# Splitting the experts' weight pieces in one operation per engine, in place of two halves

## The chip, the cores and the metric

One core of one Trainium2 chip runs the whole program. The metric is device time in microseconds (us), the median of several runs. The reader needs five engines' names: TensorE (PE, with its weight loads shown apart as PEld), VectorE (DVE), ScalarE (ACT), GpSimd (POOL) and SyncE (SP), which issues the weight loads from HBM.

## What is computed

The reference is two small transformer models, one after the other, on 256 tokens of width 1024, all in fp32. Each has two layers of mixing (recurrences and several attentions) and feed-forward. What matters here is the last feed-forward, a mixture of 8 experts with two experts per token:

```python
out = jnp.zeros_like(t)
for e in range(N_EXPERTS):
    out = out + combine[:, e:e + 1].astype(t.dtype) * swiglu(t, wg[e], wu[e], wd[e])
```

with `swiglu(x, wg, wu, wd) = (silu(x @ wg) * (x @ wu)) @ wd`; `wg` and `wu` are 1024 x 3584 and `wd` is 3584 x 1024 per expert. The kernel gathers each expert's tokens (at most 128) and so reads all 8 experts' weights once.

## The kernel before, in words

**Pieces.** All weights of the program are cut into 565 pieces of at most 128 partitions x 2048 columns (1 MB), in the order of use (`plan`). The experts' pieces are 336 of them: for each expert 7 groups of 512 hidden columns, and for each group two pieces "g" (gate), two pieces "u" (up) and two pieces "d" (down, of the group before). Their key begins with "moe".

**Precision.** TensorE multiplies fp32 operands as high and low parts. ScalarE copies a piece into `WH` (the high part, fp32r; line 1670 of the kernel), VectorE subtracts it from the raw piece into `WL` (the low part; line 2250), and TensorE makes three products for each block (`mm3`, lines 772 to 774): high by high, low by high, high by low. A piece of an expert takes 12 matmuls of 512 columns. The inputs are `XTH`/`XTL` for "g" and "u", and `HTH`/`HTL` for "d".

**Buffers and queues.** `WH` and `WL` hold WR = 3 pieces each. The raw pieces have 5 slots (`raw`), and 5 more lent ones (in `AR`) during the experts. SP issues the load of a slot's next piece when the second half of `WL` of the slot's last piece is made (line 598).

**The order on each engine.** Every engine runs its instructions in the order in which they were written. A helper, `Lane`, writes the split of piece i+2 where the engine comes to piece i (`take`), as two halves: `split(i, 0)` and `split(i, 1)`, each with its own wait and its own increment of the semaphores `wh` and `wl`. In the experts' part the two halves always stand one behind the other. ScalarE's first half waits for the landed load and for `wdone(i-3)`, TensorE's last matmul on the buffer that it overwrites. VectorE's half waits for the same half of `WH`. TensorE waits for `wl(i, 0)` ahead of a piece and for `wl(i, 1)` ahead of its second part.

**What stands between the splits.** In group i of the experts, ScalarE and VectorE have besides:
- ScalarE copies the transposed hidden block into `HTH` (L2068), ahead of the split of a second "u" piece; VectorE subtracts for `HTL` (L2914).
- ScalarE's Silu of the gate (L2092), ahead of the split of a first "d" piece; VectorE's product with the up part (L2941), ahead of the split of a first "g" piece.
- once per expert, `put_back` (L2072 on ScalarE, L2919 on VectorE), which takes an expert's result from PSUM; and `prep` of the next expert, whose two sets of four small copies (L2051 on ScalarE, L2893 on VectorE) make its `XTH` and `XTL`.
- in the last expert, after groups 3 and 5, `unfold` on VectorE (L2876): two operations of 128x1024 that add the gathered sums to `X`.
- in the first expert, the places of the rows (a string of tiny VectorE operations, L2841 to L2850 among them).

Of the kernel before, what the change touches and what calls it, by code (L numbers as in the profile page):

```python
# [7 lines left out]
F32 = mybir.dt.float32  # L8
# [4 lines left out]
ALU = mybir.AluOpType  # L13
# [8 lines left out]
WR = 3  # L22
# [6 lines left out]
class Sig:  # L29
# [9 lines left out]
    def inc(self, *key):  # L39
        assert self.keys[self.n] == key, (self.sem.name, self.keys[self.n], key)  # L40
        self.n += 1
        return self.sem, 1


    def part(self, name):

        return Part(self, name)
# [193 lines left out]
def program(nc, dr, cf, cb, ci, out):  # L241
    ctx = ExitStack()
    with ctx:
        def sb(name, shape, dt=F32):
            return ctx.enter_context(nc.sbuf_tensor(name, shape, dt))

        def sem(name):
            return ctx.enter_context(nc.semaphore(name))

        def sig(name, *keys):  # L250

            if len(keys) == 1 and isinstance(keys[0], list):
                return Sig(sem("s_" + name), keys[0])
            return Sig(sem("s_" + name), itertools.product(*[range(k) if isinstance(k, int) else k for k in keys]))
# [3 lines left out]
        WH = sb("WH", [P, WR, 2048], F32R)  # L258
        WL = sb("WL", [P, WR, 2048], F32R)
# [126 lines left out]
        for l in range(2):  # L386
            for key, ap, n in ((("n1", l), dr["norm1_g"], 8), (("n2", l), dr["norm2_g"], 8), (("nm", l), dr["norm_mix_2"], 8),
# [3 lines left out]
                if key != ("n1", 0):  # L391
                    k = sum(v[1] for v in rows.values())
# [11 lines left out]
        PIECES = plan(dr)  # L404
# [8 lines left out]
        slots = [raw[:, i, :] for i in range(RAW)] + lent  # L413


        ld_w = [sem(f"ld_w{s}") for s in range(RAW + LENT)]
        wh = sig("wh", NP, 2)
        wl = sig("wl", NP, 2)
        wdone = sig("wdone", NP)
        tops = {("m1", 0), ("m1", 1), ("m2", 0)}  # L420
        tdone = sig("tdone", [(i,) for key, i in sorted(final.items(), key=lambda x: x[1])
                              if key[0] != "moe" and (key[0] not in tops or key[1] != "d" or key[2] == (5 if key[0][0] == "m2" else 7))])
# [1233 lines left out]
        def scalar():  # L1656
            act = nc.scalar
            own = Own(sem("a_step"))

            def split(i, h):  # L1660
                s, k, _, _ = HOME[i]
                m = PIECES[i][2] * PIECES[i][3]
                c = slice(h * m // 2, (h + 1) * m // 2)
                if i == 0:
                    act.wait_ge(*((ld_w[s], 16) if h else (ld_h, 16)))
                elif h == 0:
                    act.wait_ge(ld_w[s], 16 * k)
                    if i >= WR:
                        act.wait_ge(*wdone.at(i - WR))
                act.copy(WH[:, i % WR, c], slots[s][:, c]).then_inc(*wh.inc(i, h))  # L1670

            lane = Lane(PIECES, split)

            def half(key, h, gains, hi=XTH, nch=4, b0=6, only=(0, 1)):
# [155 lines left out]
            for r in range(2):  # L1830
                half(("n1", 0), 0, gain4(("n1", 0), 0), only=(r,))
                split(0, r)
            half(("n1", 0), 1, gain4(("n1", 0), 1), b0=0)
            split(1, 0)
            split(1, 1)
            norm(("n1", 0), (ld_x, 16), (ld_y, 16))
# [11 lines left out]
            for l in range(2):  # L1848
# [32 lines left out]
                for t in range(T):  # L1881
                    m = act.activation(XN[:, t, :], XN[:, t, :], ACT.Sigmoid)
# [5 lines left out]
                for t in range(T):  # L1888
                    m = act.activation(ZB[:, t, :], ZB[:, t, :], ACT.Sigmoid)
# [351 lines left out]
        def vector():  # L2241
            dve = nc.vector
            own = Own(sem("v_step"))

            def split(i, h):
                s, _, _, _ = HOME[i]
                m = PIECES[i][2] * PIECES[i][3]
                c = slice(h * m // 2, (h + 1) * m // 2)
                dve.wait_ge(*wh.at(i, h))
                dve.tensor_tensor(WL[:, i % WR, c], slots[s][:, c], WH[:, i % WR, c].bitcast(F32), ALU.subtract).then_inc(*wl.inc(i, h))  # L2250

            lane = Lane(PIECES, split, True)

            def half(key, h, gains, hi=XTH, lo=XTL, nch=4, b0=6, only=(0, 1)):
# [250 lines left out]
            for r in range(2):  # L2505
                half(("n1", 0), 0, gain4(("n1", 0), 0), only=(r,))
                split(0, r)
            half(("n1", 0), 1, gain4(("n1", 0), 1), b0=0)
            split(1, 0)
            split(1, 1)  # L2510
            lane.cut = 2
# [703 lines left out]
```

## Time and profile before

| what | value |
|---|---|
| time, median of 3 runs | 2423.18 us (2423.03 to 2423.38) |
| profiled execution, span from first to last instruction | 2422.9 us |
| TensorE busy | 2397.3 us, 99% of the span |
| VectorE busy | 1753.7 us, 72% |
| ScalarE busy | 1493.6 us, 62% |
| experts' part | about 1437 to 2386 us |
| moved from and to HBM | 612 MB, mean 253 GB/s |

The profile puts each instruction under its line and engine. "Busy" of TensorE is modelled and includes the tail of each matmul, which overlaps the next. The mean of an operation (in ns) is from its start to its acknowledged end, and operations queued back to back overlap by about 0.1 us. "Idle before" is the time in which an engine had nothing running ahead of an instruction, with what released it. The granted clock is the share of 2.4 GHz that TensorE had.

### The profile page before, as it was taken

To read this page: it belongs to the slowest core of one execution; us is meant where nothing else is said; L and a number is where in the kernel's file an instruction comes from. 1 tells how busy PE (TensorE), PEld (TensorE's weight loads), DVE (VectorE), ACT (ScalarE), POOL (GpSimd) and SP (SyncE) were. 2 spreads that over 40 slices of the span, in tenths; PEclk is the share of its full clock that TensorE was granted. 3 is DMA by queue.
4 is the path that set the end of the run, shared out by engine and by line. 5 is a ranking of instruction groups with operands and counts; after the bars stand their busy time and mean duration, and the time that the engine had idled before them with its cause. 6 is when DMAs were issued, how large, how long until landed. Compare 5 with 4: busy or idle time off the path is not lost.

```text
span 2422.9 us, 30793 instructions
## 1 busy us (share of the span) xinstructions
PE 2397.3 (99%) x12268; PEld 2028.3 (84%) x12268; DVE 1753.7 (72%) x2133; ACT 1493.6 (62%) x1951; POOL 85.0 (4%) x106
## 2 busy tenths in 40 slices
PE   9999999999999999999999999999999999999998
PEld 7888899888888998888888888888888888888887
DVE  5655655566456556565455579999999999999997
ACT  5445544544454445554446667787777777877776
POOL 0000000000000000110000200000000000000000
PEclk9999999999999999999999999999999999999999
DMA  8453575544546555345555369999999999999992
GB/s 302 143 175 123 173 253 186 186 157 142 171 139 197 191 183 166 122 162 190 165 184 173 122 250 389 394 389 379 385 379 384 380 385 377 384 380 379 380 389 97
DMA packets 267984, 612.10 MB, mean 253 GB/s; under 512 B 12424, under 2 KB 17526, under 8 KB 267836
## 3 DMA queue, kind: packets, MB, share of 16 engines
q1 hardware_dynamic: 263356, 594.38, 69.2%
q0 software_dynamic: 4320, 15.49, 1.6%
q8 instruction: 100, 1.64, 0.3%
q14 instruction: 48, 0.39, 0.0%
q10 hardware_dynamic: 160, 0.20, 0.0%
HBM read 599.26 MB, written 11.01 MB: 252 GB/s over the span
## 4 chain that ended last, share of the span: by engine, by line
PE 93%; DVE 4%; DMA 1%; ACT 1%; POOL 1%; issue 1%; SPq 0%; POOLq 0%; ACTq 0%; DVEq 0%
PE PS L772 24%; PE PS L774 24%; PE PS L773 23%; PE PS L831 3%; PE PS L827 3%; PE PS L829 2%; DVE WL L2250 2%; PE PS L760 1%; PE PS L753 1%; PE PS L755 1%; PE PS L919 1%; PE PS L1376 1%; PE PS L883 1%; PE PS L874 1%; PE PS L989 1%; PE PS L958 1%
## 5 line engine op out<-in xcount | busy, mean ns | idle before, releaser
L2250 DVE TENSOR_TENSOR WL<-raw,WH 128x1024 fp32r<-128x1024 f32 (+2 forms) x796 | 930.2, 1209 | 300.7 <-ACT WH L1670 295.4
L1670 ACT CAST WH<-raw 128x1024 fp32r<-128x1024 f32 (+2 forms) x796 | 792.4, 1042 | 327.7 <-PE PS L774 283.5
L772 PE MATMUL PS<-WH,XTH 128*128 128x512 f32 (+2 forms) x1952 | 771.9, 395 | 0.6 <-DVE WL L2250 0.5
L774 PE MATMUL PS<-WH,XTL 128*128 128x512 f32 (+2 forms) x1952 | 755.4, 387 | 0.0
L773 PE MATMUL PS<-WL,XTH 128*128 128x512 f32 (+2 forms) x1952 | 753.8, 386 | 0.0
L774 PEld LDWEIGHTS PS<-WH,XTL 128*128 128x128 f32 x1952 | 366.6, 188 | 76.0
L772 PEld LDWEIGHTS PS<-WH,XTH 128*128 128x128 f32 x1952 | 367.0, 188 | 73.8 <-issue 2.7
L773 PEld LDWEIGHTS PS<-WL,XTH 128*128 128x128 f32 x1952 | 367.4, 188 | 69.0
L2250 DVE TENSOR_TENSOR WL<-AR,WH 128x1024 fp32r<-128x1024 f32 x334 | 391.6, 1220 | 26.9 <-ACT WH L1670 26.0
L1670 ACT CAST WH<-AR 128x1024 fp32r<-128x1024 f32 x334 | 334.3, 1052 | 66.0 <-PE PS L774 65.8
L772 PE MATMUL PS<-WH,HTH 128*128 128x512 f32 x706 | 275.1, 390 | 1.5 <-issue 1.5
L774 PE MATMUL PS<-WH,HTL 128*128 128x512 f32 x706 | 274.8, 389 | 0.0
L773 PE MATMUL PS<-WL,HTH 128*128 128x512 f32 x706 | 274.8, 389 | 0.0
L772 PEld LDWEIGHTS PS<-WH,HTH 128*128 128x128 f32 x706 | 132.5, 188 | 29.4 <-issue 1.7
L774 PEld LDWEIGHTS PS<-WH,HTL 128*128 128x128 f32 x706 | 132.5, 188 | 27.6
L773 PEld LDWEIGHTS PS<-WL,HTH 128*128 128x128 f32 x706 | 132.5, 188 | 27.4
L827 PE MATMUL PS<-XTH,WH 128*128 128x256 f32 x512 | 144.0, 283 | 0.0
L831 PE MATMUL PS<-XTH,WL 128*128 128x256 f32 x512 | 143.8, 283 | 0.0
L829 PE MATMUL PS<-XTL,WH 128*128 128x256 f32 x480 | 135.9, 283 | 0.0
L827 PEld LDWEIGHTS PS<-XTH,WH 128*128 128x128 f32 x512 | 98.2, 192 | 0.7
L831 PEld LDWEIGHTS PS<-XTH,WL 128*128 128x128 f32 x512 | 98.2, 192 | 0.0
L829 PEld LDWEIGHTS PS<-XTL,WH 128*128 128x128 f32 x480 | 92.1, 192 | 0.5
(350 smaller groups left out, 1978.3 us busy)
## 6 DMA issues: line engine op xcount, KB each, us to landing
raw<-in_w_in SPq DMA_DIRECT2D x91, 1024.0 KB, 5.2
raw<-in_moe_w_gate SPq DMA_DIRECT2D x57, 1024.0 KB, 7.8
raw<-in_moe_w_up SPq DMA_DIRECT2D x57, 1024.0 KB, 8.0
AR<-in_moe_w_down SPq DMA_DIRECT2D x57, 1024.0 KB, 8.1
AR<-in_moe_w_gate SPq DMA_DIRECT2D x55, 1024.0 KB, 7.7
AR<-in_moe_w_up SPq DMA_DIRECT2D x55, 1024.0 KB, 7.8
raw<-in_moe_w_down SPq DMA_DIRECT2D x55, 1024.0 KB, 8.2
raw<-in_w_up SPq DMA_DIRECT2D x32, 1024.0 KB, 5.5
```

The lines of the kernel that those rows point to most:

```text
L753: pe.matmul(o, lh(2 * c + d), a[k + d], start=start and d == 0, stop=False, skip_group_check=True)
L755: pe.matmul(o, lh(2 * c + d), b[k + d], start=False, stop=False, skip_group_check=True)
L760: m = pe.matmul(o, ll(2 * c + d), a[k + d], start=False, stop=stop and d == 1, skip_group_check=True)
L772: pe.matmul(o, lh, rh, start=start, stop=False, skip_group_check=True)
L773: pe.matmul(o, lh, rl, start=False, stop=False, skip_group_check=True)
L774: return pe.matmul(o, ll, rh, start=False, stop=stop, skip_group_check=True)
L827: pe.matmul(o[s], a[k + d][:, cs[s]], h, start=start and s + d == 0, stop=False, skip_group_check=True)
L829: m = pe.matmul(o[s], a[k + d][:, cs[s]], XTL[:, 2 * c + d, :], start=False, stop=False, skip_group_check=True)
L831: m = pe.matmul(o[s], b[k + d][:, cs[s]], h, start=False, stop=stop and d == 1, skip_group_check=True)
L874: m = pe.transpose(PS[:, b0 + r, c * 256 + t * P:c * 256 + t * P + P], src[:, t, cc * P:cc * P + P], ident)
L1670: act.copy(WH[:, i % WR, c], slots[s][:, c]).then_inc(*wh.inc(i, h))
L2250: dve.tensor_tensor(WL[:, i % WR, c], slots[s][:, c], WH[:, i % WR, c].bitcast(F32), ALU.subtract).then_inc(*wl.inc(i, h))
```

## The change

For a piece whose key begins with "moe", ScalarE makes `WH` of the whole piece in one copy of 128x2048, and VectorE makes `WL` of the whole piece in one subtraction of 128x2048. Each stands where the first half stood, and adds 2 to the semaphore in place of 1 and 1 (`Sig.both`). VectorE's operation waits for the value that the second half of `WH` had. The second half's call does nothing. TensorE's waits, SP's waits and all other pieces are as they were. The experts' part has so 336 operations fewer on each of the two engines.

```diff
+    def both(self, i):
+        self.inc(i, 0)
+        sem, _ = self.inc(i, 1)
+        return sem, 2
...
+        def whole(i):
+            return PIECES[i][0][0][0] == "moe"
...
 # ScalarE, split(i, h)
+                if whole(i):
+                    if h == 0:
+                        act.wait_ge(ld_w[s], 16 * k)
+                        act.wait_ge(*wdone.at(i - WR))
+                        act.copy(WH[:, i % WR, 0:m], slots[s][:, 0:m]).then_inc(*wh.both(i))
+                    return
...
 # VectorE, split(i, h)
+                if whole(i):
+                    if h == 0:
+                        dve.wait_ge(*wh.at(i, 1))
+                        dve.tensor_tensor(WL[:, i % WR, 0:m], slots[s][:, 0:m], WH[:, i % WR, 0:m].bitcast(F32),
+                                          ALU.subtract).then_inc(*wl.both(i))
+                    return
```

## Rows read from the trace of the kernel before

**Rows 1.** The page's chain that ended last: shares of the span by engine

```profile
PE 93%; DVE 4%; DMA 1%; ACT 1%; POOL 1%; issue 1%; SPq 0%; POOLq 0%; ACTq 0%; DVEq 0%
```

**Rows 2.** Experts' stretch: busy us of PE, PEld, DVE, ACT, POOL; clock; DMA

```profile
1440.00:2386.00 946.00, 944.27 (x4306) 781.67 (x4305) 874.74 (x871) 740.75 (x845) 22.57 (x24) 1.00 1.01 377
```

**Rows 3.** Waits of PEld and of SP, 1440 to 2386: us, times, longest

```profile
PEld PS L772 <- DVE WL L2250: 0.4, 1, 0.4
...
SPq L598 <- DVE WL L2250: 805.6, 327, 12.3
```

**Rows 4.** The two splits by shape: count, busy us, mean ns, idle before

```profile
L2250 DVE TENSOR_TENSOR WL<-raw,WH 128x1024 fp32r<-128x1024 f32 x780 | 919.8, 1220 | 286.8 <-ACT WH L1670 281.5 <-issue 3.1
L2250 DVE TENSOR_TENSOR WL<-raw,WH 128x512 fp32r<-128x512 f32 x8 | 5.2, 686 | 8.3 <-ACT WH L1670 8.3
...
L1670 ACT CAST WH<-raw 128x1024 fp32r<-128x1024 f32 x780 | 783.2, 1050 | 309.0 <-PE PS L774 264.7 <-PE PS L831 43.1 <-DMA raw<-in_w_in 0.8
L1670 ACT CAST WH<-raw 128x512 fp32r<-128x512 f32 x8 | 4.6, 622 | 12.0 <-PE PS L774 12.0
```

**Rows 5.** Order of time, an ordinary group: start us, us, instruction, [idle]

```profile
2350.57 2.00 ACT L1670 CAST WH<-AR 128x1024 fp32r<-128x1024 f32 x2
2353.35 1.99 ACT L1670 CAST WH<-AR 128x1024 fp32r<-128x1024 f32 x2
...
2354.42 4.66 DVE L2250 TENSOR_TENSOR WL<-AR,WH 128x1024 fp32r<-128x1024 f32 x4 [0.41 <-ACT WH L1670]
...
2357.42 0.39 PE L772 MATMUL PS<-WH,XTH 128*128 128x512 f32 x1
...
2357.87 0.19 PEld L772 LDWEIGHTS PS<-WH,HTH 128*128 128x128 f32 x1
2358.10 0.39 PE L772 MATMUL PS<-WH,HTH 128*128 128x512 f32 x1
```

**Rows 6.** Order of time, a group with the next expert's small copies

```profile
1603.06 2.01 ACT L1670 CAST WH<-raw 128x1024 fp32r<-128x1024 f32 x2
...
1606.54 0.68 DVE L2914 TENSOR_TENSOR HTL<-PS,HTH 128x512 fp32r<-128x512 f32 x1
...
1608.17 4.62 DVE L2250 TENSOR_TENSOR WL<-raw,WH 128x1024 fp32r<-128x1024 f32 x4
...
1613.44 0.19 PEld L772 LDWEIGHTS PS<-WH,HTH 128*128 128x128 f32 x1
```

**Rows 7.** Order of time, a group with an expert's result taken from PSUM

```profile
1572.12 2.01 ACT L1670 CAST WH<-raw 128x1024 fp32r<-128x1024 f32 x2
...
1578.94 0.19 PEld L772 LDWEIGHTS PS<-WH,HTH 128*128 128x128 f32 x1
```

**Rows 8.** Order of time, the last expert's group with unfold

```profile
2322.03 2.01 ACT L1670 CAST WH<-AR 128x1024 fp32r<-128x1024 f32 x2 [0.29 <-PE PS L774]
...
2325.39 0.68 DVE L2941 TENSOR_TENSOR AR<-PS,AR 128x512 f32<-128x512 f32 x1
...
2328.51 5.76 DVE L2250 TENSOR_TENSOR WL<-AR,WH 128x1024 fp32r<-128x1024 f32 x5
...
2329.78 0.19 PEld L772 LDWEIGHTS PS<-WH,XTH 128*128 128x128 f32 x1
```

**Rows 9.** Order of time, the experts' start

```profile
1439.80 3.93 ACT L1670 CAST WH<-raw 128x1024 fp32r<-128x1024 f32 x4
...
1442.90 0.19 PEld L772 LDWEIGHTS PS<-WH,XTH 128*128 128x128 f32 x1
...
1461.01 2.36 DVE L2250 TENSOR_TENSOR WL<-raw,WH 128x1024 fp32r<-128x1024 f32 x2
...
1462.42 0.19 PEld L772 LDWEIGHTS PS<-WH,HTH 128*128 128x128 f32 x1
...
1463.42 0.19 PEld L772 LDWEIGHTS PS<-WH,HTH 128*128 128x128 f32 x1 [0.36 <-DVE WL L2250]
```

**Rows 10.** The page's DMA issues: count, KB each, us to landing

```profile
AR<-in_moe_w_down SPq DMA_DIRECT2D x57, 1024.0 KB, 8.1
```

## The prediction

> **What bounds the kernel now.** I read the chain that ended last first: 93% of the span is TensorE, 4% VectorE [rows 1]. The stretches come next. In the experts' part, 946 us long, TensorE has its full clock, 2.4 GHz (1.00 in the row), and is busy for 944 us, while VectorE is busy for 875 us, 92%, and ScalarE for 741 us, 78% [rows 2]. Nearly full is not full, and the waits say which engine leads: in these 946 us TensorE's weight loads waited for `WL` once, for 0.4 us [rows 3]. So a cheaper VectorE buys nothing by itself. What can cost is lateness: any moment at which a piece's `WL` comes after TensorE wants it is added to the end, because TensorE has no idle time in which to catch up. The loads are no bound either: SP waited 805.6 us for `WL` of the slots' last pieces [rows 3], so it is the slots that pace them, not the transfers. The question is thus how late `WL` comes after the change, place by place, and how early it comes now.
>
> TensorE's pace: three matmuls from 2357.42 to 2358.10 [rows 5], 0.227 us each, so a piece of 12 takes 2.72 us.
>
> **The price of the whole operations.** The trace has no 128x2048 form, so I extend the two shapes that it has [rows 4]. VectorE: 686 ns for 512 columns, 1220 for 1024, so 534 ns for each further 512, and 1220 + 2 x 534 = 2288 ns for 2048. ScalarE: 622 and 1050 ns, 428 for each further 512, and 1906 ns for 2048. Two halves run for 2.36 us on VectorE and 2.00 on ScalarE [rows 9, 5], so each engine is relieved of 0.07 and 0.09 us per piece. That relief is worth nothing where TensorE leads.
>
> The delay is larger. Now VectorE begins about 1.07 us after ScalarE (2354.42 against 2353.35 [rows 5]), when the first half of `WH` is there; the second half follows at once, and with the pair's run of 2.36 us [rows 9] the piece is complete 3.43 us after ScalarE's start. Afterwards the chain is 1.91 + 0.03 + 2.29 = 4.23 us, 0.8 later. The 0.03 is the handover between the two engines: 1.07 less a copy's mean of 1.05 [rows 4], rounded up. Handing over to TensorE takes 0.05: at 2328.51 + 1.22 = 2329.73 a half was ready, at 2329.78 TensorE's load began [rows 8]. In all 4.28 us from ScalarE's start to TensorE's. TensorE, which now needs only the first half to begin (2.34 us in the same count), will begin a piece 1.9 us later wherever it is waiting already, and wherever it isn't, the slack decides.
>
> **The ordinary groups: nothing.** A first "d" piece: ScalarE starts at 2353.35 and TensorE wants the piece at 2357.87, the first load for `HTH` [rows 5]. The room is 4.52 us against 4.28: 0.24 to spare. The "u" piece ahead of it: ScalarE at 2350.57, wanted one piece earlier, at 2357.87 - 2.72 = 2355.15; room 4.58, 0.30 to spare. These two are the tightest of the six pieces of a group, and the pattern repeats in nearly all 56 groups. The other four pieces have 0.5 us or more after the shift, VectorE's work in between (`HTL`, the product) counted.
>
> **The next expert's small copies: +2.8 us.** `prep`'s second set stands on both engines ahead of a second "u" piece [rows 6]. With whole operations the piece before it starts on ScalarE at 1603.06 and is complete on VectorE at 1603.06 + 4.23 = 1607.29, so `HTL` begins at 1607.21 (operations overlap by 0.08). From `HTL`'s start to `WL`'s is 1608.17 - 1606.54 = 1.63, so `WL` begins at 1608.84 and is seen by TensorE at 1611.18. It is wanted at 1613.44 - 2.72 = 1610.72. Late by 0.46 us. I walked through all seven preparations: six are late by 0.46 to 0.48, the seventh just in time. 6 x 0.47 = 2.8 us.
>
> **An expert's result taken from PSUM: +1.3 us.** ScalarE's copy L2072 pushes the split behind it to 1572.12 [rows 7]; plus 4.28 is 1576.40, wanted at 1578.94 - 2.72 = 1576.22. Late by 0.18 to 0.2, seven times: 1.3 us.
>
> **The last expert's `unfold`: +3.7 us.** Here VectorE is the late one [rows 8]. The piece ahead starts on ScalarE at 2322.03 and is complete at 2326.26 in place of 2325.46; the product begins at 2326.18 in place of 2325.39. From there to the next `WL` is 3.12 us as now, so 2329.30, and the whole subtraction with its handover ends at 2331.64. TensorE started on the first half at 2329.78. Late by 1.86 us, and it happens twice (groups 3 and 5), 3.7 us.
>
> **The start: +1.7 us.** ScalarE comes to the third expert piece at 1439.80; plus 4.28 is 1444.08, wanted at 1442.90 [rows 9]: 1.2 us. Some pieces later VectorE is behind because of the row places: the subtraction that began at 1461.01 would end at 1463.30, wanted at 1462.42, 0.9 late, but today's wait of 0.36 before its second half goes: 0.5 us net.
>
> **Loads.** A slot is released 0.8 us later. The releases keep their pace of one in 2.8 us (946 us for 336 pieces), and ten slots are in turn, so a slot comes round in 28 us; a load lands 8.1 us after its issue [rows 10] and the splits take some 5, which leaves about 15 us to spare. Starting 0.8 us later costs nothing.
>
> **The sum.** 2.8 + 1.3 + 3.7 + 1.7 = 9.5 us on the profiled execution's span of 2422.9, which is 0.3 under the median of the runs; on that median, 2432.7 us.
>
> **Bounds.** The unknown is the price of a whole operation. From below: a half has a fixed part of 1220 - 1068 = 152 ns on VectorE and 194 on ScalarE; if all of it were saved off the pair's run, the whole would take 2.21 and 1.81, the chain 4.10. Each of the late places then shrinks (`prep` to 0.2, the result to 0.03, `unfold` to 1.6, the start to 1.1): 5.7 us in all. From above, two halves' full durations, 2.44 and 2.10: the chain is 4.62, and the ordinary groups' 0.24 and 0.30 to spare are gone; they lose about 0.1 us each, and the special places grow: 20 us. I take the extended shapes, as they are the same operation with more columns.
>
> The Trainium skill, Perfetto Trace Analysis, section Optimizing Scalar/DVE Operations, says two things that part here: grouping work into larger operations helps if the engine is saturated, and if it isn't saturated but makes bubbles on other engines, breaking instructions up lets work finish sooner. The first would make this change a gain (the rival below), the second makes it a loss. The waits above side with the second.
>
> **Rivals.**
> - *VectorE is what paces the experts* (faster). For it: 92% busy. Then 336 x 0.07 = 24 us would go and the time would be 2399. Against: it decides only if TensorE waits for `WL` in most pieces, and it waits 0.4 us in all. 3%.
> - *Only the large places show* (same). If the whole operations are 0.1 to 0.2 us shorter in the chain than I take them and TensorE's queued instructions hide the rest, `prep` and the results cost nothing and a little over 4 us is left from `unfold` and the start: 2427.5. For it: these overshoots are 0.2 to 0.5 us only. Against: a late piece in today's rows does show in TensorE. 10%.
> - *The change does nothing*, all the delay hidden: 2423.2. Against: the two `unfold` places have no slack today. 3%.
> - *Every group pays* (slower still). If a whole operation costs as two halves, or the handover is longer after long operations, 0.3 us more in the chain turn the ordinary groups late: 2443. For it: the slack of 0.24 is the difference of large numbers. 9%.
>
> **How the numbers follow.** The forecast has 75%; its own range is 2429 to 2437. The range for 8 in 10 reaches down to the second rival, 2427.5, and up to 2440, short of the last rival's full price. Faster by over 0.2% (4.8 us, about what a measurement of this kernel can tell from no change) is the first rival, 3%; within 0.2% are the second and third, 13%; slower, 84%.
>
> **What would show it.** In the profile after: `WL` of 128x2048 at about 2290 ns and `WH` at 1910; PEld or PE waiting for the whole `WL` some 17 times in the experts' part, about 10 us in total, with 1.2 near the third piece, 0.2 and 0.5 once per expert, and two of nearly 2 us in the last; VectorE's busy time in the experts' part lower by some 24 us and its idle time for `WH` higher; the time before 1437 us unchanged. I am wrong if TensorE waits in ordinary groups, if a whole operation is far from the extended price, or if TensorE's waits are there but the time isn't.

## The result: 12 us slower, and the profile after

| | before | after |
|---|---|---|
| time, median of 5 runs | 2423.18 us (2423.03 to 2423.73) | 2435.43 us (2435.14 to 2435.98) |
| span of the profiled execution | 2422.9 us | 2434.7 us |

The ratio is 1.0051, with a 95% interval from 1.004 to 1.0062: slower by 12.25 us, where 9.5 was forecast. I read the views of the kernel after in the order of [rows 1 to 5]. First the page's chain that ended last, by engine:

```profile
PE 88%; DVE 6%; ACT 2%; issue 1%; DMA 1%; POOL 1%; SPq 0%; DVEq 0%; ACTq 0%; POOLq 0%
```

TensorE's share fell from 93% to 88%. Next the experts' stretch, with the columns of [rows 2], 12.3 us longer at its end:

```profile
1440.00:2398.30 958.30, 949.81 (x4311) 781.14 (x4310) 854.71 (x536) 712.09 (x512) 29.82 (x24) 1.00 1.00 372
```

TensorE's clock is still the upper level, 2.4 GHz (1.00). VectorE has 20 us less work than in [rows 2] and ScalarE 29 less, and the stretch is longer all the same. GpSimd (the last pair of columns with a count) is busy for 29.82 us with the same 24 instructions, 7.3 more than in [rows 2]; that turns out to matter. The waits of TensorE's weight loads in the experts' part (us in total, times, longest):

```profile
PEld PS L782 <- DVE WL L2268: 12.1, 18, 2.1
PEld PS L1334 <- DMA AR<-expert_rows: 1.9, 1, 1.9
PEld PS L782 <- DVE HTL L2936: 1.5, 1, 1.5
PEld PS L1451 <- DVE HTL L2987: 1.3, 1, 1.3
PEld PS L782 <- issue: 0.6, 1, 0.6
```

One wait for `WL` of 0.4 us [rows 3] has become 18 of 12.1 us together. The whole operations, as in [rows 4]:

```profile
L2268 DVE TENSOR_TENSOR WL<-raw,WH 128x2048 fp32r<-128x2048 f32 x169 | 386.4, 2291 | 51.4 <-ACT WH L1678 50.7
...
L1678 ACT CAST WH<-raw 128x2048 fp32r<-128x2048 f32 x169 | 323.9, 1917 | 78.5 <-PE PS L784 78.5
```

2291 and 1917 ns, against 2288 and 1906 forecast. The Trainium skill (VectorE: DVE Perf Modes, section The TRN2 errata) gives for an fp32 `tensor_tensor` add of N columns (N+151)/0.96 ns, which is 2291 for 2048; for this subtraction the trace agrees to the nanosecond, and at 512 and 1024 columns it has 686 and 1220 [rows 4] where the formula gives 691 and 1224.

**Place by place.** Both kernels issue the same 12268 matmuls in the same order, so each one's start after can be set against its start before. The difference is flat, then steps, then flat again; the steps say where time went. In us (forecast, measured):

| place | forecast | after |
|---|---|---|
| start of the experts, three steps | 1.7 | 1.23 + 0.45 + 0.44 = 2.12 |
| wait for the second expert's gathered rows | none | 1.26 |
| small copies, six steps | 2.8 | 2.87 |
| result from PSUM, seven steps | 1.3 | 1.33 |
| `unfold`, two steps | 3.7 | 1.95 + 1.89 = 3.84 |
| end of the experts' part | none | 0.63 |
| all ordinary groups | 0 | 0 |

The steps sum to 12.05, and those at the four places of the forecast to 10.16, where 9.5 was forecast. The wait for the rows, which the forecast put at nothing, is the largest part of what is missing. Before 1437 us the kernel after is 0.5 us ahead, which it gains some 6 us after the first instruction, in code that didn't change; the last matmuls are 11.5 apart, the spans 11.8, the medians 12.25.

The steps in the order of time (start us, us, instruction, [idle before]). The third piece of the experts' start:

```profile
1439.29 3.75 ACT L1678 CAST WH<-raw 128x2048 fp32r<-128x2048 f32 x2
...
1441.34 4.49 DVE L2268 TENSOR_TENSOR WL<-raw,WH 128x2048 fp32r<-128x2048 f32 x2 [1.71 <-ACT WH L1678]
...
1443.68 0.19 PEld L782 LDWEIGHTS PS<-WH,XTH 128*128 128x128 f32 x1 [1.32 <-DVE WL L2268]
```

VectorE stands idle for 1.71 us until the whole `WH` is there, and only then starts. A group with an expert's result taken from PSUM, the answer to [rows 7]:

```profile
1575.49 1.92 ACT L1678 CAST WH<-raw 128x2048 fp32r<-128x2048 f32 x1
...
1577.52 4.59 DVE L2268 TENSOR_TENSOR WL<-raw,WH 128x2048 fp32r<-128x2048 f32 x2 [0.56 <-ACT WH L1678]
...
1579.59 0.39 PE L784 MATMUL PS<-WH,XTL 128*128 128x512 f32 x1
1579.87 0.19 PEld L782 LDWEIGHTS PS<-WH,XTH 128*128 128x128 f32 x1 [0.32 <-DVE WL L2268]
```

And the first `unfold`, the answer to [rows 8]:

```profile
2333.92 2.60 DVE L2898 SCALAR_TENSOR_TENSOR X<-AR,sm,X 128x1024 f32<-128x1024 f32 x2
...
2336.44 4.49 DVE L2268 TENSOR_TENSOR WL<-AR,WH 128x2048 fp32r<-128x2048 f32 x2
...
2338.77 0.19 PEld L782 LDWEIGHTS PS<-WH,XTH 128*128 128x128 f32 x1 [2.06 <-DVE WL L2268]
```

The subtraction that starts at 2336.44 must run its full 2.29 us ahead of TensorE's load, where [rows 8] shows the load 1.27 us after it.

### The profile page after: what moved, and what is told of

Same layout as the page of the kernel before. It is cut to its first block, busy times and chain, and to the rows that moved or that the text cites. A ratio compares the mean times of both kernels' runs of the same rounds, so it can differ in the third digit from the quotient of the medians.

```text
span 2434.7 us, 30456 instructions
## 1 busy us (share of the span) xinstructions
PE 2401.6 (99%) x12268; PEld 2026.8 (83%) x12268; DVE 1733.1 (71%) x1797; ACT 1464.2 (60%) x1615; POOL 93.7 (4%) x106
## 4 chain that ended last, share of the span: by engine, by line
PE 88%; DVE 6%; ACT 2%; issue 1%; DMA 1%; POOL 1%; SPq 0%; DVEq 0%; ACTq 0%; POOLq 0%
PE PS L782 23%; PE PS L784 22%; PE PS L783 22%; PE PS L841 3%; PE PS L837 3%; PE PS L839 2%; DVE WL L2268 2%; PE PS L770 1%; PE PS L763 1%; PE PS L765 1%; PE PS L929 1%; DVE WL L2272 1%; ACT WH L1678 1%; PE PS L893 1%; PE PS L1386 1%
## 5 line engine op out<-in xcount | busy, mean ns | idle before, releaser
L2272 DVE TENSOR_TENSOR WL<-raw,WH 128x1024 fp32r<-128x1024 f32 (+2 forms) x458 | 534.6, 1202 | 276.4 <-ACT WH L1686 273.7
L1686 ACT CAST WH<-raw 128x1024 fp32r<-128x1024 f32 (+2 forms) x458 | 453.9, 1033 | 263.3 <-PE PS L784 218.8
L2268 DVE TENSOR_TENSOR WL<-raw,WH 128x2048 fp32r<-128x2048 f32 x169 | 386.4, 2291 | 51.4 <-ACT WH L1678 50.7
L2268 DVE TENSOR_TENSOR WL<-AR,WH 128x2048 fp32r<-128x2048 f32 x167 | 382.0, 2291 | 49.5 <-ACT WH L1678 49.0
L1678 ACT CAST WH<-raw 128x2048 fp32r<-128x2048 f32 x169 | 323.9, 1917 | 78.5 <-PE PS L784 78.5
L1678 ACT CAST WH<-AR 128x2048 fp32r<-128x2048 f32 x167 | 319.9, 1915 | 79.9 <-PE PS L784 79.9
```

What stands on the lines that cost most here:

```text
L1678: act.copy(WH[:, i % WR, 0:m], slots[s][:, 0:m]).then_inc(*wh.both(i))
L2268: dve.tensor_tensor(WL[:, i % WR, 0:m], slots[s][:, 0:m], WH[:, i % WR, 0:m].bitcast(F32), ALU.subtract).then_inc(*wl.both(i))
```

## The experiments

My theory is that of the prediction: the loss is the lateness of a complete `WL` at some 17 places without slack, and nothing elsewhere. The rivals: a price paid in every group, one of the two engines' changes alone, and something else of the long operations. Results, each beside the kernel before on the same chip (us):

| run | median (lowest to highest) | above before | ratio, 95% interval |
|---|---|---|---|
| act_whole | 2425.71 (2425.25 to 2426.07) | +2.67 | 1.0011, 1.0002 to 1.002 |
| dve_whole | 2436.59 (2436.25 to 2437.75) | +13.55 | 1.0057, 1.0043 to 1.0071 |
| no_start | 2431.05 (2430.56 to 2431.22) | +8.01 | 1.0033, 1.002 to 1.0045 |
| no_late | 2424.14 (2423.61 to 2424.98) | +1.10 | 1.0004, 0.9995 to 1.0013 |
| parts_3 | 2433.67 (2433.24 to 2434.11) | +10.34 | 1.0043, 1.0029 to 1.0056 |
| parts_8 | 2443.33 (2443.02 to 2444.04) | +20.00 | 1.0083, 1.007 to 1.0097 |
| late_only | 2436.50 (2436.25 to 2438.56) | +13.05 | 1.0056, 1.0043 to 1.007 |
| changed_again | 2435.20 (2434.59 to 2435.59) | +11.75 | 1.0049, 1.0036 to 1.0063 |

The same comparison of matmuls, each kernel against the trace of before (us):

| place | after | changed_again | act_whole | dve_whole | no_start | no_late | parts_3 | parts_8 | late_only |
|---|---|---|---|---|---|---|---|---|---|
| start | 2.12 | 2.08 | 0.84 | 2.24 | 0.0 | 0.0 | 2.37 | 2.55 | 2.10 |
| rows | 1.26 | 1.16 | -0.47 | 1.25 | -0.45 | -0.47 | -0.45 | -0.25 | 1.39 |
| copies | 2.87 | 2.82 | 0.0 | 3.41 | 2.60 | 0.49 | 2.86 | 2.98 | 2.86 |
| results | 1.33 | 1.34 | 0.0 | 1.98 | 1.42 | 0.0 | 1.36 | 1.73 | 1.33 |
| `unfold` | 3.84 | 3.85 | 1.73 | 3.96 | 3.84 | 0.57 | 3.87 | 4.01 | 3.82 |
| end | 0.63 | -0.21 | 0.05 | -0.29 | -0.50 | -0.42 | -0.41 | -0.24 | 0.90 |
| ordinary groups | 0 | 0 | 0 | 0 | 0 | 0 | 0 | 8.70 | 0 |

All columns are set against one traced execution of before, and that one was itself about 1 us longer than usual. Its span is 2422.9 us; 40 later executions of the same kernel have spans of 2421.3 to 2423.0, with a median of 2421.8. So the columns sum to 0.2 to 1.1 us less than the medians show. The negative entries, 0.45 at the rows and some 0.4 at the end in kernels that have no reason to gain there, are most likely time that this execution of before lost. All nine kernels are also 0.2 to 0.7 us ahead of it at 1437 us, where their code is the same.

### act_whole: only ScalarE's copy is whole

```diff
 # VectorE, split(i, h)
                 if whole(i):
-                    if h == 0:
-                        dve.wait_ge(*wh.at(i, 1))
-                        dve.tensor_tensor(WL[:, i % WR, 0:m], slots[s][:, 0:m], WH[:, i % WR, 0:m].bitcast(F32),
-                                          ALU.subtract).then_inc(*wl.both(i))
+                    dve.wait_ge(*wh.at(i, 1))
+                    dve.tensor_tensor(WL[:, i % WR, c], slots[s][:, c], WH[:, i % WR, c].bitcast(F32), ALU.subtract).then_inc(*wl.inc(i, h))
                     return
```

> ScalarE's copy of an expert piece stays whole, VectorE's subtraction is made again in two halves, both of which wait for the whole copy. Theory (lateness: what costs is only the moment at which TensorE gets the first part of WL at some 18 places): the first half is there 1.91 + 0.03 + 1.22 + 0.05 = 3.2 us after ScalarE's start, against 2.3 in the kernel before and 4.3 in the changed one. The places with the next expert's copies and with the result taken from PSUM have the room for that and cost nothing again; the two unfold places keep some 0.9 us each, the start 0.1 to 0.6: 2425 to 2427 us. Rival (fewer, longer operations cost in themselves, through ScalarE as much as through VectorE): half of the loss stays, 2429 us or more. Besides: GpSimd's indirect transfers at the experts' start took 2.4 us each in the changed kernel and 1.2 before. If it is VectorE's long operations that hold them up they are back at 1.2 here, if ScalarE's, they stay at 2.4.

It lost 2.67 us. The late start of VectorE alone costs only where nothing covers 0.8 us: the start and the two `unfold` (0.88 and 0.85). TensorE can still begin on a first half, and the small copies and results cost nothing.

### dve_whole: only VectorE's subtraction is whole

```diff
 # ScalarE, split(i, h)
-                if whole(i):
-                    if h == 0:
...
-                        act.copy(WH[:, i % WR, 0:m], slots[s][:, 0:m]).then_inc(*wh.both(i))
-                    return
```

> VectorE's subtraction of an expert piece stays whole, ScalarE's copy is made again in two halves. Lateness: VectorE begins when the second half of WH is there, 0.08 us later than with the whole copy, so the start, the seven results from PSUM and the two unfold places are late by 0.08 more each, the rest as in the changed kernel: 2436 us, 0.5 to 1 above the changed kernel. Rival (half of the loss belongs to ScalarE's long copies): 2429 us. GpSimd's indirect transfers stay at 2.4 us if VectorE's operations hold them up.

It lost 13.55, more than the full change: VectorE waits for the second of two copies, which is complete 0.08 us later than one whole copy, and each late place grew by 0.1 (copies 3.41 for six, results 1.98 for seven). So the loss is VectorE's whole subtraction handed over as one; ScalarE's whole copy, beside it, gives 0.1 us per late place back. That is 1.3 us above the change's 12.25, where I expected 0.5 to 1: I had not counted the small copies.

### no_start: halves for the first 19 pieces of the experts

```diff
-            return PIECES[i][0][0][0] == "moe"
+            return PIECES[i][0][0][0] == "moe" and i >= first[("moe", "g", 0, 0)] + 19
```

> As the changed kernel, but the first 19 pieces of the experts' part are split in halves. Lateness: the start's 1.2 and 0.8 us go, and so does TensorE's wait of 1.25 us for the rows of the second expert, if it came from the late start and from GpSimd's slow indirect transfers: 3.2 us less than the changed kernel, 2432.2. Rival (each whole piece costs the same): 19 of 336 pieces, 0.7 us less, 2434.7. Rival for the wait for rows (the load of the rows is late for another reason, the traffic of the pieces' loads): that wait of 1.25 stays, 2433.4.

The loss is 8.01 us against the change's 12.25, 4.2 less, where I expected 3.2 less. In the profiled executions the spans differ by 5.0: the start's 2.1 are gone, as they should be, and most of the rest is the wait for the gathered rows, 1.7 us less and so not only back to its value in before but under it, and 1.1 at the end. At the other late places it pays as the kernel after does.

### no_late: 296 of the 336 pieces whole, none where it is late

```diff
-            return PIECES[i][0][0][0] == "moe"
+            key, kp = PIECES[i][0]
+            if key[0] != "moe" or i < first[("moe", "g", 0, 0)] + 19:
+                return False
+            _, kind, e, n = key
+            if kind == "u" and kp == 1 and n in (1, 3):
+                return False
+            return (kind, e, n, kp) not in [("d", 7, 2, 0), ("d", 7, 2, 1), ("g", 7, 4, 0), ("d", 7, 4, 0), ("d", 7, 4, 1), ("g", 7, 6, 0)]
```

> As the changed kernel, but halves at the places where TensorE waited: the first 19 pieces, the second u piece of groups 1 and 3 of each expert, and the six pieces around the two unfold operations. 297 or so of 336 pieces stay whole. Lateness: TensorE waits nowhere, and the time is that of the kernel before to within 1 us (0.6 may stay at the very end, where TensorE waited for HTL after the branch, if that has to do with the change): 2423.2 to 2424.2. Rival (each whole piece costs the same): 10.8 of the 12.2 us stay, 2434. A rival of the other sign (the VectorE and ScalarE time saved is worth something once the late places are gone): below 2422.5.

It lost 1.10 us; the interval takes in no change. The table places 1.06 of it: 0.49 at the small copies, six steps of about 0.08, and 0.57 around the `unfold` places, where TensorE still waits 0.44 us for a half of `WL`. So 40 pieces in halves take back all but about 1 us of the 12.25, and the expected "TensorE waits nowhere" was not quite met. VectorE's splits in the experts' part:

```profile
L2274 DVE TENSOR_TENSOR WL<-raw,WH 128x2048 fp32r<-128x2048 f32 x149 | 340.5, 2290 | 42.5 <-ACT WH L1684 41.7 <-issue 0.4
L2274 DVE TENSOR_TENSOR WL<-AR,WH 128x2048 fp32r<-128x2048 f32 x147 | 336.3, 2290 | 45.7 <-ACT WH L1684 45.3
L2278 DVE TENSOR_TENSOR WL<-raw,WH 128x1024 fp32r<-128x1024 f32 x44 | 51.5, 1217 | 2.5 <-issue 1.7 <-ACT WH L1692 0.8
```

With 296 whole subtractions and 1.1 us lost, where a price for each whole piece would have left 10.8, such a price is out; and with 296 fewer operations on each engine and nothing won, so is a gain from fewer operations.

### parts_3 and parts_8: the first "d" piece of each group in 3 or 8 subtractions, with one signal at the end

```diff
                         dve.wait_ge(*wh.at(i, 1))
+                        if PIECES[i][0][0][1] == "d" and PIECES[i][0][1] == 0:
+                            cuts = [j * m // 3 // 64 * 64 for j in range(3)] + [m]
+                            for a, b in zip(cuts, cuts[1:]):
+                                op = dve.tensor_tensor(WL[:, i % WR, a:b], slots[s][:, a:b], WH[:, i % WR, a:b].bitcast(F32), ALU.subtract)
+                            op.then_inc(*wl.both(i))
+                            return
```

(parts_8 has 8 for 3.) These ask whether the ordinary groups really have about 0.24 us to spare: three operations take longer than one by less than that, eight by more.

> As the changed kernel, but VectorE makes the WL of each first d piece in three operations behind one another with one signal at the end, so that the piece is complete 2 x 0.07 = 0.14 us later. In the ordinary groups the forecast found 0.24 us to spare at just this piece. If so, nothing there, and only the unfold places and some neighbours pay 0.1 each: 0 to 0.6 us above the changed kernel, 2435.4 to 2436.0. If the spare time is less than forecast (TensorE needs the piece earlier than its load begins), some 45 places x 0.1 = 4 us or more above.

> As the kernel with three operations, but with eight: the first d piece is complete 7 x 0.07 = 0.49 us later. That is 0.25 more than the spare time of 0.24 us, at some 50 places: 12 us above the changed kernel, 2447, with TensorE waiting in every group. Rival (VectorE is paced by something else, or the waits of TensorE are no part of the time): within 1 us of the changed kernel.

The cut pieces in parts_3 and in parts_8, in the order of time:

```profile
2362.79 2.43 DVE L2271 TENSOR_TENSOR WL<-AR,WH 128x640 fp32r<-128x640 f32 x3 [0.39 <-ACT WH L1678]
```

```profile
2372.12 2.10 DVE L2271 TENSOR_TENSOR WL<-AR,WH 128x256 fp32r<-128x256 f32 x6 [0.41 <-ACT WH L1678]
```

Three take 2.43 us, 0.14 more than one, and no ordinary group lost anything. In the second row six take 2.10; at 0.42 each and a step of (2.10 - 0.42) / 5 = 0.336, eight take 2.77, 0.48 more than one. TensorE's weight loads in parts_8:

```profile
PEld PS L782 <- issue: 16.1, 48, 1.1
PEld PS L782 <- DVE WL L2274: 12.1, 19, 2.1
```

The 12.1 us of waits for whole pieces are there as in the kernel after, and 48 new ones besides. (The profile calls them "issue"; they stand at the cut pieces, and no other kernel has more than 6 of them.) The matmuls step by 0.21 us in each ordinary group, 8.70 us in all. So a group covers 0.48 - 0.21 = 0.27 us and no more. I expected 0.25 lost per place and a time of 2447: the mechanism held, the count and the size were both a little less.

parts_3 came out 1.8 us *faster* than the kernel after, though it only adds operations; I had expected 0 to 0.6 us slower. The table shows where: the wait for the gathered rows, -0.45 in place of 1.26, and the end. That put GpSimd in question.

### late_only: whole at the 47 pieces where it is late, halves everywhere else

```diff
-            return PIECES[i][0][0][0] == "moe"
+            key, kp = PIECES[i][0]
+            if key[0] != "moe":
+                return False
+            if i < first[("moe", "g", 0, 0)] + 19:
+                return True
+            _, kind, e, n = key
+            if kind == "u" and (n == 3 or n == 1 and kp == 1):
+                return True
+            return (kind, e, n, kp) in [("d", 7, 2, 0), ("d", 7, 2, 1), ("g", 7, 4, 0), ("d", 7, 4, 0), ("d", 7, 4, 1), ("g", 7, 6, 0)]
```

> The reverse of the kernel with halves at the late places: 47 of the 336 expert pieces are whole (the first 19, both second-matrix pieces of group 3 and the last one of group 1 of each expert, six around the two unfold operations), all others are halves as in the kernel before. Lateness: the same late places pay as in the changed kernel, 10 to 12 us above the kernel before, 2433 to 2435, with one seventh of the whole operations. Rival (each whole piece costs the same): 47/336 of 12.2, 1.7 us, 2425.

47 of 336 pieces, 14%, make the whole loss: 13.05 us, in the same steps. The expected range ended 1.5 us lower. The profiled execution has 0.90 at the end (below); the rest is not placed.

### changed_again: the changed kernel once more

No edit.

> The changed kernel itself, a second profile and five rounds. Open is a wait of TensorE near the end of its first profile, 0.8 us longer than before, that two kernels with whole subtractions there did not show. If it is part of the kernel it stands in this profile again and the time is 12.2 us above the kernel before. If it belongs to single executions, this profile has it or not, and the waits before it are the same to 0.1 us.

All steps come back within 0.1 us, but for the end: +0.63 there, -0.21 here.

## Why the prediction was right, and what it missed

The mechanism was right: lateness of `WL` at places without slack. The measured loss is 2.75 us larger than the forecast because two terms were short: what waits on GpSimd was put at nothing, and the start was mis-sized.

**What bounds the kernel, and the prices: right.** No gain from less work on VectorE, 1.00 of the clock, 2291 and 1917 ns for the whole operations. VectorE's relief was 20 us, not 24: where pieces follow each other at once, four halves took 4.66 us [rows 5] and two wholes 4.60, 0.03 a piece, and 0.07 only where a pair stands alone.

**Ordinary groups, small copies, results, `unfold`: right.** 0, 2.87, 1.33 and 3.84 us against 0, 2.8, 1.3 and 3.7, and no_late and late_only show from both sides that these places and the start are the loss. Two errors hid in this agreement. The chain from ScalarE's start to TensorE's is 1579.87 - 1575.49 = 4.38 us in the row above, not 4.28: VectorE begins 0.1 us after a whole copy ends, not 0.03. And TensorE covers as much: its load is due one step ahead of its matmul, so at 1579.59 there, and came 0.28 late, yet the matmuls step by 0.19 at this place. The wait in brackets is so no measure of the loss; the next matmuls are. The spare time in ordinary groups has the same two parts, about 0.17 up to the load and 0.1 beyond it, together the 0.27 of parts_8.

One reading beside the sum was wrong too: the span of 2422.9 is not that of an execution 0.3 us under the median. In every run for which both are on record the time is 1.25 to 1.85 us above the span, mostly 1.3, so the traced execution took about 2424.2. The forecast difference does not depend on it.

**The start: mis-sized, 2.12 for 1.7.** The third piece was right (1.2, measured 1.23). At 1460 to 1464 us I took 0.5 net for one piece; two pieces were late, 0.45 and 0.44. I had walked the subtraction behind the row places and not the one in front of it.

**Nothing for what waits on GpSimd: wrong, 1.26 us.** The term "Loads" counted only the weight pieces. The second expert's rows are first written to `expert_rows` by four indirect DMAs of GpSimd, and the instructions that issue them take longer beside whole subtractions. Before, then after, GpSimd and VectorE's splits in the order of time:

```profile
1457.64 2.35 DVE L2250 TENSOR_TENSOR WL<-AR,WH 128x1024 fp32r<-128x1024 f32 x2
1458.68 1.18 POOL L680 DMA_INDIRECT expert_rows<-XN,IDX  x1 [26.09 <-DVE IDX L2866]
...
1460.16 0.98 POOL L680 DMA_INDIRECT expert_rows<-XN,IDX  x1 [0.30 <-issue]
...
1461.45 1.62 POOL L680 DMA_INDIRECT expert_rows<-XN,IDX  x1 [0.31 <-issue]
```

```profile
1458.56 2.29 DVE L2268 TENSOR_TENSOR WL<-AR,WH 128x2048 fp32r<-128x2048 f32 x1
1459.60 2.26 POOL L690 DMA_INDIRECT expert_rows<-XN,IDX  x1 [27.52 <-DVE IDX L2888]
...
1461.92 2.29 DVE L2268 TENSOR_TENSOR WL<-raw,WH 128x2048 fp32r<-128x2048 f32 x1
1462.16 2.90 POOL L690 DMA_INDIRECT expert_rows<-XN,IDX  x1 [0.30 <-issue]
...
1464.73 4.48 DVE L2268 TENSOR_TENSOR WL<-raw,WH 128x2048 fp32r<-128x2048 f32 x2
1465.37 2.48 POOL L690 DMA_INDIRECT expert_rows<-XN,IDX  x1 [0.30 <-issue]
1468.15 1.91 POOL L690 DMA_INDIRECT expert_rows<-XN,IDX  x1 [0.30 <-issue]
```

The four take 9.5 us in place of 4.7, and the last ends at 1470.06 in place of 1464.33. The load of the rows is issued at 1477.74 in place of 1474.14: 7.68 us behind the last one, where it was 9.81. TensorE's wait for it grew from 0.7 to 1.9 us:

```profile
1485.71 0.42 PEld L1334 LDWEIGHTS PS<-CF,AR 128*128 128x128 f32 x4 [1.94 <-DMA AR<-expert_rows]
```

The runs side with this. Where VectorE has halves at this place (act_whole, no_start, no_late), the four instructions take 1.18 to 1.19 us on the mean, as in before, and TensorE doesn't wait for the rows (in before it waited 0.7 us; there the load was issued 9.81 us after the last indirect DMA, against 9.29 in no_start and 9.10 in act_whole, so that wait most likely belongs to the transfers of this one execution, and the change's price here is nearer to 1.7 us than to 1.26); where the subtractions are whole (after, changed_again, dve_whole, late_only) 2.38 to 2.39, and it waits 1.8 to 2.1; with some pieces cut (parts_3, parts_8) 1.91 and 1.95, and it doesn't wait. It follows VectorE's change, not ScalarE's: act_whole has the whole copies too. Nor is it the late start: parts_3 starts as late as the kernel after (2.37 us) and doesn't wait.

**The end: not forecast, partly open.** +0.63 after, +0.90 in late_only, under zero in six of the others. The waits there:

```profile
2397.30 0.69 ACT L2127 ACTIVATE HTH<-PS,sm 128x512 fp32r<-128x512 f32 x1 [2.89 <-PE PS L784]
...
2398.86 0.75 DVE L2987 SCALAR_TENSOR_TENSOR HTL<-PS,sm,HTH 128x512 fp32r<-128x512 f32 x1 [2.11 <-ACT HTH L2127]
2399.66 0.19 PEld L1451 LDWEIGHTS PS<-HTL,PTH 128*128 128x128 f32 x1 [1.29 <-DVE HTL L2987]
```

VectorE began 2398.86 - (2397.30 + 0.69) = 0.87 us after its input was there; in changed_again, at the same place:

```profile
2396.99 0.69 ACT L2127 ACTIVATE HTH<-PS,sm 128x512 fp32r<-128x512 f32 x1 [2.87 <-PE PS L784]
2397.71 0.75 DVE L2987 SCALAR_TENSOR_TENSOR HTL<-PS,sm,HTH 128x512 fp32r<-128x512 f32 x1 [1.35 <-ACT HTH L2127]
```

0.03 us. The same kernel has it in one execution and not in another, so it is no part of the change's price in every run; what held VectorE back stays open. What the change costs is best taken from the medians, 12.25 and 11.75 us. The two spans of changed_again and before lie only 10.3 apart, but the first was the shortest of its five runs and the second about 1 us longer than usual.

**The rivals.** VectorE as the pace (2399) is refuted by no_late: 296 operations fewer on each engine, no gain. "Only the large places show" failed because the small ones paid to within 0.1 us of their lateness. "Every group pays" was nearer than its price says: the slack that kept it away is 0.27 us, and parts_8 shows that 0.48 us more in one piece of a group turns it on.

## What to carry to other kernels

When TensorE has no idle time, halves are a hand-over and not an overhead: a merged operation saved 0.03 to 0.09 us on an engine that had time to spare, and delivered its first part up to 1.9 us later wherever the producer had no slack. Walk the places that have extra work between producer and consumer; 47 of 336 pieces made the whole loss, and halves at 40 of them gave back all but about 1 us. Ask also who else works beside the lengthened instruction: here it was GpSimd, whose delay came out at a TensorE wait 20 us later.

## What the runs showed of the hardware

GpSimd's indirect DMA instructions wait for VectorE's subtraction. By the rows above, one that starts with no subtraction running takes 0.98 us (at 1460.16). One that starts while one runs ends 0.83 to 1.01 us after that subtraction's end, as if it only then began. Worked out from these rows (a single operation of a pair by its mean):

| kernel | indirect DMA, start to end | the subtraction's end | ends after it by |
|---|---|---|---|
| before | 1458.68 to 1459.86 | 1457.64 + 1.22 = 1458.86 | 1.00 |
| before | 1461.45 to 1463.07 | 1461.01 + 1.22 = 1462.23 [rows 9] | 0.84 |
| after | 1459.60 to 1461.86 | 1458.56 + 2.29 = 1460.85 | 1.01 |
| after | 1462.16 to 1465.06 | 1461.92 + 2.29 = 1464.21 | 0.85 |
| after | 1465.37 to 1467.85 | 1464.73 + 2.29 = 1467.02 | 0.83 |
| after | 1468.15 to 1470.06 | 1464.73 + 4.48 = 1469.21 | 0.85 |

In these rows it waits for the one that is running and not for the next: in the first row of before the second half began at once, and the instruction ended while that half ran. So here the length of a single VectorE operation sets the delay, not how busy VectorE is. The second set of four, `AR<-expert_sums` near the end, goes the same way: in before and after, seven of the eight start while a subtraction runs and end 0.86 to 0.94 us after it, and the mean rose from 1647 to 2258 ns. One of the 80 in the ten traces did not get in between. In late_only it stood beside six halves in a row and ended 0.91 us after the fourth of them:

```profile
2301.16 4.80 POOL L720 DMA_INDIRECT AR<-expert_sums,IDX  x1 [0.30 <-issue]
```

```profile
2300.43 7.01 DVE L2280 TENSOR_TENSOR WL<-AR,WH 128x1024 fp32r<-128x1024 f32 x6
```

Why this one waited for four stays open.

GpSimd's other work isn't held up; in the kernel after:

```profile
L690 POOL DMA_INDIRECT expert_rows<-XN,IDX x4 | 9.5, 2387 | 28.4 <-DVE IDX L2888 27.5 <-issue 0.9
L699 POOL DMA_DIRECT2D AR<-expert_rows x7 | 3.8, 546 | 47.3 <-DMA expert_sums<-AR 39.6 <-DMA expert_rows<-XN,IDX 7.7
L707 POOL MEMSET AR<- 128x2048 f32 x2 | 3.7, 1826 | 33.2 <-DVE X L2898 33.2
```

Before, the same three took 1184, 545 and 1826 ns. Both memsets and most of the direct DMAs had a whole subtraction running beside them in the kernel after.

A VectorE operation with only one input in SBUF did not hold the indirect DMA up. The product with the up part reads PSUM and SBUF; in the kernel before:

```profile
1463.29 0.68 DVE L2941 TENSOR_TENSOR AR<-PS,AR 128x512 f32<-128x512 f32 x1
1463.37 0.96 POOL L680 DMA_INDIRECT expert_rows<-XN,IDX  x1 [0.30 <-issue]
```

The DMA started 0.08 us into the product and took no longer than alone: it ended at 1464.33, 0.36 us after the product's end at 1463.97. act_whole, no_start and no_late show the same, 0.96 to 0.97 us. The Trainium skill (SBUF — State Buffer, section Who interferes with whom) says that a VectorE instruction with two SBUF inputs contends with a GpSimd instruction that reads SBUF, and not with one that only writes it, and it calls the port pair that the two engines share an exclusive lock. The trace agrees in all that it can show: the subtraction has two SBUF inputs, the indirect DMA reads its list of indices, the memset only writes, and the product with one SBUF input holds nothing up. But the product is also shorter than the subtraction (0.68 us), and no run here takes the second SBUF input away from the same operation, so that the port is the cause is made likely and not shown by itself.
